# Position-bias lines of a hybrid decoder trunk: all heads in one matmul, sixteen partitions per head, written to memory in one transfer

## The chip, the cores and the metric

The kernel runs on one core of one Trainium2 chip. A core has a matrix engine (TensorE, PE in the tables, with its weight loads listed apart as PEld), a vector engine (DVE), a scalar engine (ACT), a GpSimd engine (POOL) and a queue processor that issues transfers (SP). 16 DMA engines move data between on-chip memory (SBUF) and HBM. The metric is the device time of one execution in microseconds; lower is better. Times "before" are the median of 3 runs.

## The reference

Two layers of a decoder trunk on 256 tokens of width 1024, all in float32: RMSNorm, one wide input projection, causal differential attention with 8 heads, a short gated convolution, an output projection, then a feed-forward part (dense in layer 0, 8 experts with top-2 routing in layer 1). The change concerns one small input of the attention, the relative-position bias, which depends only on the head and on the distance between query and key:

```python
dists = jnp.arange(S, dtype=jnp.int32)
bias_dist = rel_bias.astype(jnp.float32)[t5_causal_bucket(dists)].T      # (heads, 256)
...
dist = qpos[:, None] - kpos[None, :]
bias = bias_dist[:, jnp.maximum(dist, 0)]
s = jnp.einsum('bqhmd,bkhmd->bhmqk', qblk.astype(jnp.float32) * scale, kf)
s = s + bias[None, :, None]
s = jnp.where(dist >= 0, s, -jnp.inf)
p = jax.nn.softmax(s, axis=-1)
```

## The kernel before

**Weights and the main loop.** The weights stream through SBUF in pieces of 1 MB, called halves (128 partitions x 2048 float32). A mixer layer has 44 halves, numbered s = 0 to 43; two of them make the weights of one output unit (the first two units are the q and k columns of four heads). SP loads a half into one of RAW = 6 slots of `w_raw` (`load_half`, L359 to L362); from half 6 on it first waits for `lo_ready`, which says that the half six places back has been split. ACT copies a half to `w_hi` (L398) and DVE, or in two places POOL, subtracts to get `w_lo` (L407): a float32 product is made of three matmuls on the two parts (`product`, L411 to L413). There are SPLIT = 3 slots for the parts, so ACT splits half n only when PE has finished half n - 3 (`half_used`). PE takes 24 matmuls of 128x512 for a half (2 token tiles x 4 chunks x 3 products).

**What sets the order.** Everything is written out by hand, one program for each engine; engines meet only at semaphores. ACT's program of mixer step s begins with the split of half s + 2; then come copies of finished results from PSUM (L804 writes q to `rows` after half 1) and jobs of the attention. PE's program of step s is the 24 matmuls and then the jobs of table `JOBS`; the first is `turn_qk` 0 after half 2, eight transposes (L1660) of the `rows` that L804 writes, into banks 4 and 5.

**The bias.** It is made once, at the start of layer 0. SP loads `relb` (32 buckets x 8 heads) and `bucket` (33 x 384, one-hot: which bucket belongs to each of 384 distances; row 32 stands for masked places and carries -1e30). DVE copies `relb` to `relb_bc` in `v_buf`, each head's column repeated 128 times (L1551). After half 1, PE transposes the taps of the convolution (`conv_rows`, L1575, bank 4) and makes for each head one float32 matmul (L1583) of `relb_bc[:, h, :]` (33 x 128, all 128 columns alike) with `bucket`; the result is the line of 384 biases of that head, the same on all 128 partitions. Heads use banks 4 to 7 twice. ACT copies each line to `bias` (L714) and the taps to `convT` (L717); PE's matmul for head h, from head 4 on, waits until ACT has copied head h - 4 (`line_sb`). After four heads and after eight, ACT issues a transfer of 4 x 128 lines to the HBM tensor `lines` (L721), waits for the small sum of the lambdas (L724), and goes on. SP waits for both transfers (`line_out`, L494), then reads `lines` back with a skewed pattern (L496), so that partition p gets its line shifted by p, which is the bias tile of each head, and after that goes on with the load of half 8. The biases are first used at step 8 by DVE (L1171).

Of the kernel before, what the change touches and what calls it, by code (L numbers as in the profile page):

```python
# [26 lines left out]
P = 128  # L27
# [4 lines left out]
ACT = mybir.ActivationFunctionType  # L32
# [5 lines left out]
KC = D // P  # L38
HEADS = 8
HD = 64  # L40
NBUCKETS = 32
EPS = 1e-6
DEPTH = 2
# [12 lines left out]
WIDE = EXPERTS // 2  # L56
NARROW = P // 2
LINE = 384
BIG = 1e30

MIX_HALVES = 44
# [81 lines left out]
def build(nc, x, rel_bias, mix_norm_g, lam_qk, subln_g, conv_w, ffn_norm_g, router_w, final_norm_g,  # L143
          mix_slabs, dense_slabs, expert_slabs, bucket_of, out):
    lines = nc.dram_tensor("bias_lines", (HEADS, P, LINE), F32, kind="Internal").ap()
    with ExitStack() as ctx:
# [18 lines left out]
        part = sb("part", [P, TT * CHUNK])  # L165
        prob = sb("prob", [P, 2, LINE])
        wgt = sb("wgt", [P, LINE])
        wgtT = sb("wgtT", [P, LINE])
        arow = sb("arow", [P, TT, P])
        squares = sb("squares", [P, TT, P])  # L170

        with ExitStack() as trunk:
# [5 lines left out]
            v_buf = shared("v_buf", [P, KC * SEQ])  # L178
            bias = shared("bias", [P, HEADS, LINE])
            uT = shared("uT", [P, 4, SEQ + 2])  # L180
# [11 lines left out]
        relb = sb("relb", [64, HEADS])  # L192
        gsub = sb("gsub", [P, DEPTH, P])
        conv_rows = sb("conv_rows", [DEPTH * 3 * KC, P])
        convT = sb("convT", [P, DEPTH, 3, KC])
# [42 lines left out]
        bank = [ctx.enter_context(nc.psum_tensor(f"bank{b}", [P, CHUNK], F32)) for b in range(8)]  # L238
# [20 lines left out]
        gain = yT[:, :]  # L259
        yTv = yT[:, :].rearrange("p (c t) -> p c t", t=SEQ)  # L260

        relb_bc = v_buf[0:64, 0:HEADS * P].rearrange("b (h p) -> b h p", p=P)
        bucket = prob[0:NBUCKETS + 1, 0, :]
        lam_flat = k_buf[:, 0:DEPTH * 4 * HD]
        lamq = lam_flat.rearrange("p (l i d) -> p l i d", l=DEPTH, i=4)
# [25 lines left out]
        line_out, bias_in, out_sent = sem("line_out"), sem("bias_in"), sem("out_sent")  # L291
# [5 lines left out]
        conv_ps, conv_sb = sem("conv_ps"), sem("conv_sb")  # L297
        sum_ps = sem("sum_ps")
        line_ps, line_sb, relb_ready = sem("line_ps"), sem("line_sb"), sem("relb_ready")
# [178 lines left out]
        def _(sp):  # L478
# [12 lines left out]
            for s in range(3, RAW + 2):  # L491
                load_half(sp, s, mixer_source(0, s))

            sp.wait_ge(line_out, 16 * 2)  # L494
            for c0, j0, n in ((0, SEQ - 1, P), (P, SEQ - 1 - P, 2 * P)):
                sp.dma_start(bias[:, :, c0:c0 + n],  # L496
                             bass.AP(tensor=lines.tensor, offset=j0,
                                     ap=[[LINE - 1, P], [P * LINE, HEADS], [1, n]])).then_inc(bias_in, 16)
            for s in range(RAW + 2, MIX_HALVES):
# [209 lines left out]
        def _(act):  # L709
            def bias_lines():  # L710

                for h in range(HEADS):
                    act.wait_ge(line_ps, h + 1)
                    act.activation(bias[:, h, :], bank[4 + h % 4][:, 0:LINE], ACT.Copy).then_inc(line_sb, 1)  # L714
                    if h == 0:
                        act.wait_ge(conv_ps, 1)
                        act.activation(convT[:, :, :, :].rearrange("p l w c -> p (l w c)"),  # L717
                                       bank[4][:, LINE:LINE + DEPTH * 3 * KC], ACT.Copy).then_inc(conv_sb, 1)
                    if h % 4 == 3:
                        act.wait_ge(line_sb, h + 1)  # L720
                        act.dma_start(lines[h - 3:h + 1].rearrange("h p j -> p h j"),  # L721
                                      bias[:, h - 3:h + 1, :]).then_inc(line_out, 16)
                act.wait_ge(lam_sums, 1)
                act.activation(lam4[:, :, :], lam4[:, :, :], ACT.Exp).then_inc(lam_exp, 1)  # L724

# [364 lines left out]
        def _(dve):  # L1090
# [457 lines left out]
            chain(dve.memset(relb[NBUCKETS:64, :], -BIG))  # L1548
            norm(0)
            dve.wait_ge(relb_in, 16)  # L1550
            dve.tensor_copy(relb_bc, relb[:, :].unsqueeze(2).to_broadcast([64, HEADS, P])).then_inc(relb_ready, 1)  # L1551
            mixer(0)
            norm(1)
            dve.sem_inc(d_rows, 1)
# [15 lines left out]
        def _(pe):  # L1570
            def bias_lines():

                n = DEPTH * 3 * KC
                pe.wait_ge(conv_in, 16)
                pe.transpose(bank[4][:, LINE:LINE + n], conv_rows[:, :], ident[0:n, 0:n]).then_inc(conv_ps, 1)  # L1575
                pe.wait_ge(bucket_in, 16)
                pe.wait_ge(relb_ready, 1)
                for h in range(HEADS):
                    if h >= 4:
                        pe.wait_ge(line_sb, h - 3)  # L1580
                    if h == 4:
                        pe.wait_ge(conv_sb, 1)
                    pe.matmul(bank[4 + h % 4][:, 0:LINE], relb_bc[0:NBUCKETS + 1, h, :], bucket,  # L1583
                              start=True, stop=True).then_inc(line_ps, 1)

            def norm_turn(q, t):
                pe.wait_ge(hrow_ready, 2 * q + t + 1)
# [6 lines left out]
            def mixer(layer):  # L1594
# [15 lines left out]
                for s in range(MIX_HALVES):  # L1610
# [31 lines left out]
                    for job in JOBS[s]:  # L1642
                        kind, i = job
                        for b in JOB_BANKS[kind]:
                            if JOB_BEFORE[job, b]:
                                job_out(pe, layer, JOB_BEFORE[job, b])
                            elif layer:
                                job_out(pe, layer - 1, LAST_JOB[b])
                            else:
                                pe.wait_ge(line_sb, HEADS)  # L1650
                        head = HEADS * layer + i
                        if kind in ("turn_qk", "turn_u", "turn_b"):
                            if kind == "turn_u":
# [17 lines left out]
                        if kind == "scores":  # L1671
                            pe.wait_ge(qk_ready, 8 * layer + (4 if i < 4 else 8))
                            for m in range(2):
                                r = slice(HD * m, HD * m + HD)
                                pe.matmul(bank[4 + m][:, 0:P], qT[r, i, 0:P], kT[r, i, 0:P], start=True, stop=True)
                                pe.matmul(bank[4 + m][:, P:LINE], qT[r, i, P:SEQ], kT[r, i, 0:SEQ],
                                          start=True, stop=True).then_inc(bank_full[4 + m], 1)
# [5 lines left out]
                        if kind == "values":  # L1683
# [6 lines left out]
                                      stop=True).then_inc(bank_full[7], 1)  # L1690
# [345 lines left out]
```

## Time and profile before

| | us |
|---|---|
| median of 3 runs | 1773.92 |
| lowest, highest | 1771.62, 1774.75 |
| profiled execution | 1775.7 |
| its span, first to last instruction | 1774.0 |
| mean granted TensorE clock in it | 0.958 of full |
| TensorE busy in it | 1681.5 (95%) |

A profile is one execution, so sums are made against its span and carried over to the median as a difference. The granted clock is 1.00 for 2.4 GHz and 0.50 for 1.2 GHz. In a timeline each row gives start, duration, engine, line, operation, tile written and tiles read, shape and count; in square brackets stands the idle time of that engine before it and what ended it. Merged rows (x8 and the like) give the duration of the group; matmuls are pipelined, so the distance from one start to the next says more than a duration. A float32 matmul of the bias appears as two entries, so a row "x8" of L1583 is four heads.

### The profile page before, as it was taken

The numbers are of one execution on the slowest core, as the hardware profiler recorded it, in microseconds if no ns is written. First come the engines' busy times: TensorE is split into PE (matmuls) and PEld (weight loads), VectorE is DVE, ScalarE is ACT, GpSimd is POOL, SyncE is SP. The second block draws the span as 40 slices with busy tenths as digits, with TensorE's granted clock in tenths as the row PEclk, the third lists the DMA queues.
The fourth block names the chain that finished last, engine by engine and source line by source line (L and its number), as shares of the span: only waits on it lengthen the run. The fifth ranks groups of instructions, "written<-read, shape, count | busy, mean of one in ns | idle before, by whom it ended". The sixth has DMA issues, their size and how long they took to land.

```text
span 1774.0 us, 22510 instructions
## 1 busy us (share of the span) xinstructions
PE 1681.5 (95%) x7827; PEld 1390.1 (78%) x7827; DVE 1312.4 (74%) x1157; ACT 1118.5 (63%) x1120; POOL 202.9 (11%) x433
## 2 busy tenths in 40 slices
PE   6999999999989999979899989999899998999996
PEld 4888887888868888868687878888788877888784
DVE  4457756444454676667798989889898899888895
ACT  4456743434345567437577877778777788677784
POOL 1034331000000344128200000000000000000000
PEclk8999999999989999978999989999899999899997
DMA  6644454555535445536698989989989899999893
GB/s 271 251 167 165 177 184 150 194 182 184 188 137 176 157 166 180 189 140 266 244 420 343 407 360 370 376 335 398 421 336 380 338 374 422 361 371 369 340 400 127
DMA packets 71803, 488.67 MB, mean 275 GB/s; under 512 B 8667, under 2 KB 11948, under 8 KB 13228
## 3 DMA queue, kind: packets, MB, share of 16 engines
q1 hardware_dynamic: 69052, 483.89, 71.1%
q10 hardware_dynamic: 2672, 3.70, 0.6%
q8 instruction: 52, 0.85, 0.2%
q14 instruction: 27, 0.22, 0.0%
HBM read 484.94 MB, written 2.62 MB: 275 GB/s over the span
## 4 chain that ended last, share of the span: by engine, by line
PE 47%; DVE 8%; issue 7%; ACT 4%; POOL 3%; DMA 2%; DVEq 0%; ACTq 0%; SPq 0%; POOLq 0%
PE bank L411 13%; PE bank L413 12%; PE bank L412 12%; DVE w_lo L407 3%; DMA w_raw<-expert_slabs 2%; PE bank L1798 2%; DVE e_v L404 2%; PE bank L1819 2%; PE bank L1820 2%; ACT w_hi L398 2%; PE bank L1836 1%; DVE e_uy L407 1%; POOL wgtT L697 1%; PE bank L1826 1%; ACT hT L395 1%
## 5 line engine op out<-in xcount | busy, mean ns | idle before, releaser
L407 DVE TENSOR_TENSOR w_lo<-w_raw,w_hi 128x2048 fp32r<-128x2048 f32 x286 | 649.9, 2290 | 272.9 <-ACT w_hi L398 272.4
L398 ACT ACTIVATE w_hi<-w_raw 128x2048 fp32r<-128x2048 f32 x289 | 549.7, 1915 | 374.8 <-PE bank L413 362.8
L411 PE MATMUL bank<-w_hi,hT 128*128 128x512 f32 x912 | 365.0, 400 | 9.7 <-DVE hT L1132 8.9
L413 PE MATMUL bank<-w_hi,hT 128*128 128x512 f32 x912 | 359.0, 394 | 0.0
L412 PE MATMUL bank<-w_lo,hT 128*128 128x512 f32 x912 | 358.4, 393 | 0.0
L411 PEld LDWEIGHTS bank<-w_hi,hT 128*128 128x128 f32 x912 | 173.7, 190 | 47.9 <-DVE hT L1132 10.8
L413 PEld LDWEIGHTS bank<-w_hi,hT 128*128 128x128 f32 x912 | 173.2, 190 | 37.4
L412 PEld LDWEIGHTS bank<-w_lo,hT 128*128 128x128 f32 x912 | 174.0, 191 | 34.7
L407 DVE TENSOR_TENSOR e_uy<-w_raw,e_k 128x2048 fp32r<-128x2048 f32 x56 | 130.1, 2323 | 40.0 <-ACT e_k L398 40.0
L398 ACT ACTIVATE e_k<-w_raw 128x2048 fp32r<-128x2048 f32 x56 | 107.3, 1916 | 62.8 <-PE bank L413 33.6
L404 DVE TENSOR_TENSOR e_v<-w_raw,hT 128x2048 fp32r<-128x2048 f32 x55 | 125.8, 2287 | 16.4 <-ACT hT L395 16.1
L413 PE MATMUL bank<-w_hi,cT_lo 128*128 128x512 f32 x328 | 128.2, 391 | 0.0
L407 DVE TENSOR_TENSOR e_bias<-w_raw,e_q 128x2048 fp32r<-128x2048 f32 x55 | 125.6, 2283 | 2.8 <-ACT e_q L398 2.8
L398 ACT ACTIVATE e_q<-w_raw 128x2048 fp32r<-128x2048 f32 x55 | 105.6, 1920 | 14.9 <-PE bank L413 10.2
L395 ACT ACTIVATE hT<-w_raw 128x2048 fp32r<-128x2048 f32 x55 | 105.4, 1916 | 13.4 <-PE bank L413 6.6
L411 PE MATMUL bank<-w_hi,cT_hi 128*128 128x512 f32 x264 | 103.2, 391 | 1.5 <-DVE cT_lo L1278 1.5
L412 PE MATMUL bank<-w_lo,cT_hi 128*128 128x512 f32 x264 | 102.7, 389 | 0.0
L1836 PE MATMUL bank<-wgt,part 128*128 128x64 f32 x448 | 60.2, 293 | 22.5 <-DVE zero_r L1412 20.9
L1836 PEld LDWEIGHTS bank<-wgt,part 128*128 128x128 f32 x448 | 60.3, 211 | 26.9 <-issue 25.2
L413 PEld LDWEIGHTS bank<-w_hi,cT_lo 128*128 128x128 f32 x328 | 61.6, 188 | 13.5
L1819 PE MATMUL bank<-w_hi,hT 128*128 128x512 f32 x160 | 62.5, 391 | 0.1
L607 POOL TENSOR_SCALAR head_nw<-head_ss 128x2 f32<-128x2 f32 x16 | 6.1, 378 | 493.1 <-ACT squares L839 493.1
(340 smaller groups left out, 2815.5 us busy)
## 6 DMA issues: line engine op xcount, KB each, us to landing
w_raw<-expert_slabs SPq DMA_DIRECT2D x334, 1024.0 KB, 7.0
w_raw<-mix_slabs SPq DMA_DIRECT2D x88, 1024.0 KB, 4.8
w_raw<-dense_slabs SPq DMA_DIRECT2D x33, 1024.0 KB, 4.8
bias_lines<-bias ACTq DMA_DIRECT2D x2, 768.0 KB, 4.2
X<-in_x SPq DMA_DIRECT2D x2, 512.0 KB, 4.2
bias<-bias_lines SPq DMA_DIRECT2D x1, 1024.0 KB, 7.4
yT<-in_ffn_norm_g ACTq DMA_DIRECT2D x2, 512.0 KB, 5.4
v_buf<-expert_slabs SPq DMA_DIRECT2D x1, 1024.0 KB, 4.9
```

The source lines that it names most:

```text
L395: act.activation(hi_slot(n), in_pair(raw_of(n, early)), ACT.Copy).then_inc(hi_ready, 1)
L398: act.activation(hi_slot(n), raw_of(n, early), ACT.Copy).then_inc(hi_ready, 1)
L404: eng.tensor_tensor(in_pair(lo_slot(n)), in_pair(raw_of(n, early)), hi_slot(n), ALU.subtract).then_inc(lo_ready, 1)
L407: eng.tensor_tensor(lo_slot(n), raw_of(n, early), hi_slot(n), ALU.subtract).then_inc(lo_ready, 1)
L411: pe.matmul(dst, hi, whi, start=first, stop=False, skip_group_check=True)
L412: pe.matmul(dst, hi, wlo, start=False, stop=False, skip_group_check=True)
L413: return pe.matmul(dst, lo, whi, start=False, stop=last, skip_group_check=True)
L697: chain(pool.tensor_tensor(terms[:, :, c, :], src[:, r:r + 2, :], col_no[:, c:c + 1, :].to_broadcast([P, 2, 2 * EXPERTS]), ALU.mult))
L1798: ins = pe.matmul(bank[b][:, P * c:P * c + P], src[:, t, P * k:P * k + P], pick_r[:, t, :], start=t == 0, stop=t == TT - 1)
L1819: pe.matmul(dst, x, whi, start=first, stop=False, skip_group_check=True)
L1820: return pe.matmul(dst, x, wlo, start=False, stop=last, skip_group_check=True)
L1836: ins = pe.matmul(bank[2][:, at:at + NARROW], raw[:, P * j:P * j + P], fold[:, :], start=True, stop=True, skip_group_check=True)
```

## The change

The eight bias matmuls become one. `relb_bc` now repeats each head's column COPIES = 16 times, so that 8 heads x 16 copies fill the 128 columns of one weight tile; one matmul (bank 5) gives a tile in which partition 16h + r holds the line of head h. ACT makes one copy of it (128x384) into `bias[:, 0, :]` and issues one transfer in which each partition's line is read eight times and written to eight consecutive rows of `lines`: 16 partitions x 8 make the 128 rows of a head. `lines` ends with the contents that it had before. SP waits for one transfer. The copy of the convolution's taps now comes ahead of the line copy on ACT. PE's jobs that use banks 4 to 7 for the first time wait for the taps and for the one line copy.

```diff
--- before.py
+++ after.py
@@ -56,6 +56,7 @@
 WIDE = EXPERTS // 2
 NARROW = P // 2
 LINE = 384
+COPIES = P // HEADS
 BIG = 1e30
 
 MIX_HALVES = 44
@@ -259,7 +260,7 @@
         gain = yT[:, :]
         yTv = yT[:, :].rearrange("p (c t) -> p c t", t=SEQ)
 
-        relb_bc = v_buf[0:64, 0:HEADS * P].rearrange("b (h p) -> b h p", p=P)
+        relb_bc = v_buf[0:64, 0:P].rearrange("b (h r) -> b h r", r=COPIES)
         bucket = prob[0:NBUCKETS + 1, 0, :]
         lam_flat = k_buf[:, 0:DEPTH * 4 * HD]
         lamq = lam_flat.rearrange("p (l i d) -> p l i d", l=DEPTH, i=4)
@@ -491,7 +492,7 @@
             for s in range(3, RAW + 2):
                 load_half(sp, s, mixer_source(0, s))
 
-            sp.wait_ge(line_out, 16 * 2)
+            sp.wait_ge(line_out, 16)
             for c0, j0, n in ((0, SEQ - 1, P), (P, SEQ - 1 - P, 2 * P)):
                 sp.dma_start(bias[:, :, c0:c0 + n],
                              bass.AP(tensor=lines.tensor, offset=j0,
@@ -709,17 +710,14 @@
         def _(act):
             def bias_lines():
 
-                for h in range(HEADS):
-                    act.wait_ge(line_ps, h + 1)
-                    act.activation(bias[:, h, :], bank[4 + h % 4][:, 0:LINE], ACT.Copy).then_inc(line_sb, 1)
-                    if h == 0:
-                        act.wait_ge(conv_ps, 1)
-                        act.activation(convT[:, :, :, :].rearrange("p l w c -> p (l w c)"),
-                                       bank[4][:, LINE:LINE + DEPTH * 3 * KC], ACT.Copy).then_inc(conv_sb, 1)
-                    if h % 4 == 3:
-                        act.wait_ge(line_sb, h + 1)
-                        act.dma_start(lines[h - 3:h + 1].rearrange("h p j -> p h j"),
-                                      bias[:, h - 3:h + 1, :]).then_inc(line_out, 16)
+                act.wait_ge(conv_ps, 1)
+                act.activation(convT[:, :, :, :].rearrange("p l w c -> p (l w c)"),
+                               bank[4][:, LINE:LINE + DEPTH * 3 * KC], ACT.Copy).then_inc(conv_sb, 1)
+                act.wait_ge(line_ps, 1)
+                act.activation(bias[:, 0, :], bank[5][:, 0:LINE], ACT.Copy).then_inc(line_sb, 1)
+                act.wait_ge(line_sb, 1)
+                act.dma_start(lines.rearrange("h (r c) j -> (h r) c j", r=COPIES),
+                              bias[:, 0, :].unsqueeze(1).to_broadcast([P, P // COPIES, LINE])).then_inc(line_out, 16)
                 act.wait_ge(lam_sums, 1)
                 act.activation(lam4[:, :, :], lam4[:, :, :], ACT.Exp).then_inc(lam_exp, 1)
 
@@ -1548,7 +1546,7 @@
             chain(dve.memset(relb[NBUCKETS:64, :], -BIG))
             norm(0)
             dve.wait_ge(relb_in, 16)
-            dve.tensor_copy(relb_bc, relb[:, :].unsqueeze(2).to_broadcast([64, HEADS, P])).then_inc(relb_ready, 1)
+            dve.tensor_copy(relb_bc, relb[:, :].unsqueeze(2).to_broadcast([64, HEADS, COPIES])).then_inc(relb_ready, 1)
             mixer(0)
             norm(1)
             dve.sem_inc(d_rows, 1)
@@ -1575,13 +1573,8 @@
                 pe.transpose(bank[4][:, LINE:LINE + n], conv_rows[:, :], ident[0:n, 0:n]).then_inc(conv_ps, 1)
                 pe.wait_ge(bucket_in, 16)
                 pe.wait_ge(relb_ready, 1)
-                for h in range(HEADS):
-                    if h >= 4:
-                        pe.wait_ge(line_sb, h - 3)
-                    if h == 4:
-                        pe.wait_ge(conv_sb, 1)
-                    pe.matmul(bank[4 + h % 4][:, 0:LINE], relb_bc[0:NBUCKETS + 1, h, :], bucket,
-                              start=True, stop=True).then_inc(line_ps, 1)
+                pe.matmul(bank[5][:, 0:LINE], v_buf[0:NBUCKETS + 1, 0:P], bucket,
+                          start=True, stop=True).then_inc(line_ps, 1)
 
             def norm_turn(q, t):
                 pe.wait_ge(hrow_ready, 2 * q + t + 1)
@@ -1647,7 +1640,8 @@
                             elif layer:
                                 job_out(pe, layer - 1, LAST_JOB[b])
                             else:
-                                pe.wait_ge(line_sb, HEADS)
+                                pe.wait_ge(conv_sb, 1)
+                                pe.wait_ge(line_sb, 1)
                         head = HEADS * layer + i
                         if kind in ("turn_qk", "turn_u", "turn_b"):
                             if kind == "turn_u":
```

PE, after half 1 of the mixer of layer 0 (`bank` is PSUM, `w_hi`, `w_lo` weight parts, `hT` the normalised input, `conv_rows` the taps, `prob` the one-hot table, `v_buf` the repeated bias columns). Before:

```order
L413 MATMUL bank<-w_hi,hT 128x512
L1575 MATMUL bank<-ident,conv_rows 128x48 [waits conv_in]
L1583 MATMUL bank<-prob,v_buf 128x384 [waits relb_ready,bucket_in]
L1583 MATMUL bank<-prob,v_buf 128x384 x3
L1583 MATMUL bank<-prob,v_buf 128x384 [waits conv_sb,line_sb]
L1583 MATMUL bank<-prob,v_buf 128x384 [waits line_sb] x3
L411 MATMUL bank<-w_hi,hT 128x512 [waits lo_ready]
```

and the same place in the changed kernel:

```order
L414 MATMUL bank<-w_hi,hT 128x512
L1573 MATMUL bank<-ident,conv_rows 128x48 [waits conv_in]
L1576 MATMUL bank<-prob,v_buf 128x384 [waits relb_ready,bucket_in]
L412 MATMUL bank<-w_hi,hT 128x512 [waits lo_ready]
L413 MATMUL bank<-w_lo,hT 128x512
```

Seven bias matmuls and the two kinds of waits for ACT between them are gone from PE; half 2 stands right behind the one that is left.

ACT, between the split of halves 3 and 4 and the split of half 5 (`lam` the lambdas, `rows` the q rows that PE transposes next). Before:

```order
L398 ACTIVATE w_hi<-w_raw 128x2048 [waits half_used,landed4]
L714 ACTIVATE bias<-bank 128x384 [waits line_ps]
L717 ACTIVATE convT<-bank 128x48 [waits conv_ps]
L714 ACTIVATE bias<-bank 128x384 [waits line_ps] x3
L721 DMA bias_lines<-bias 128x4x384 [waits line_sb]
L714 ACTIVATE bias<-bank 128x384 [waits line_ps] x4
L721 DMA bias_lines<-bias 128x4x384 [waits line_sb]
L724 ACTIVATE lam<-lam 128x4 [waits lam_sums]
L804 ACTIVATE rows<-bank 128x512 [waits half_used]
L804 ACTIVATE rows<-bank 128x512
L398 ACTIVATE w_hi<-w_raw 128x2048 [waits half_used,landed5]
```

and the same place in the changed kernel:

```order
L399 ACTIVATE w_hi<-w_raw 128x2048 [waits half_used,landed4]
L714 ACTIVATE convT<-bank 128x48 [waits conv_ps]
L717 ACTIVATE bias<-bank 128x384 [waits line_ps]
L719 DMA bias_lines<-bias 1024x1x384 [waits line_sb]
L722 ACTIVATE lam<-lam 128x4 [waits lam_sums]
L802 ACTIVATE rows<-bank 128x512 [waits half_used]
L802 ACTIVATE rows<-bank 128x512
L399 ACTIVATE w_hi<-w_raw 128x2048 [waits half_used,landed5]
```

Seven copies and one issue are gone from ACT ahead of the two copies of `rows`; the one transfer that is left names 1024 rows of 384 on its written side.

## Rows read from the trace of the kernel before

**Rows 1.** Busy time of each engine by stretch, with granted clock and DMA share

```profile
core 0: us, PE busy (x) PEld busy (x) DVE busy (x) ACT busy (x) POOL busy (x), PEclk, DMA share, GB/s
...
30.25:33.00 2.75, 2.75 (x10) 1.48 (x9) 0.64 (x1) 2.58 (x2) 0.00 (x0) 1.00 0.00 0
33.00:40.13 7.13, 5.58 (x9) 2.49 (x8) 3.85 (x2) 4.22 (x9) 0.00 (x0) 0.50 0.31 112
40.13:47.15 7.02, 7.02 (x26) 5.62 (x26) 0.00 (x0) 1.67 (x4) 0.00 (x0) 0.78 0.53 159
...
60.00:288.00 228.00, 228.00 (x1109) 186.73 (x1108) 141.97 (x170) 127.56 (x211) 66.66 (x152) 1.00 0.50 176
...
865.00:1774.00 909.00, 865.88 (x4043) 722.91 (x4041) 809.88 (x538) 681.90 (x525) 0.00 (x0) 0.95 0.92 363
```

**Rows 2.** Timeline of PE, from the taps' transpose to half 3

```profile
30.25 0.26 PE L1575 MATMUL bank<-ident,conv_rows 48*128 48x48 f32 x1
30.36 2.84 PE L1583 MATMUL bank<-prob,v_buf 33*128 33x384 f32 x8
34.75 5.45 PE L1583 MATMUL bank<-prob,v_buf 33*128 33x384 f32 x8 [1.55 <-ACT convT L717]
40.13 0.79 PE L411 MATMUL bank<-w_hi,hT 128*128 128x512 f32 x1
...
43.51 0.40 PE L413 MATMUL bank<-w_hi,hT 128*128 128x512 f32 x1
...
47.15 1.03 PE L1660 MATMUL bank<-ident,rows 128*128 128x128 f32 x8
...
47.94 0.48 PE L411 MATMUL bank<-w_hi,hT 128*128 128x512 f32 x1
```

**Rows 3.** Timeline of ACT, 30 to 68 us

```profile
30.42 3.71 ACT L398 ACTIVATE w_hi<-w_raw 128x2048 fp32r<-128x2048 f32 x2 [4.93 <-PE bank L413]
...
34.41 0.20 ACT L717 ACTIVATE convT<-bank 128x48 f32<-128x48 f32 x1
34.50 1.25 ACT L714 ACTIVATE bias<-bank 128x384 f32<-128x384 f32 x3
35.78 0.42 ACTq L721 DMA_DIRECT2D bias_lines<-bias  x1
...
40.76 0.38 ACTq L721 DMA_DIRECT2D bias_lines<-bias  x1
...
41.30 1.07 ACT L804 ACTIVATE rows<-bank 128x512 f32<-128x512 f32 x2
...
65.52 1.92 ACT L398 ACTIVATE w_hi<-w_raw 128x2048 fp32r<-128x2048 f32 x1 [3.44 <-PE bank L413]
```

**Rows 4.** Granted clock and DMA rate in short stretches, columns as in Rows 1

```profile
33.00:33.20 0.20, 0.20 (x1) 0.00 (x0) 0.20 (x1) 0.20 (x1) 0.00 (x0) 0.51 0.00 0
...
37.00:38.00 1.00, 1.00 (x3) 0.47 (x2) 0.00 (x0) 0.32 (x1) 0.00 (x0) 0.50 0.95 352
...
43.20:43.40 0.20, 0.20 (x2) 0.12 (x1) 0.00 (x0) 0.00 (x0) 0.00 (x0) 0.89 1.05 376
```

**Rows 5.** Timeline of DVE: split of halves 3 and 4, first use of the bias

```profile
32.36 4.49 DVE L407 TENSOR_TENSOR w_lo<-w_raw,w_hi 128x2048 fp32r<-128x2048 f32 x2 [2.72 <-ACT w_hi L398]
...
82.62 1.15 DVE L1171 TENSOR_TENSOR prob<-bank,bias 128x384 f32<-128x384 f32 x2 [1.91 <-PE bank L1676]
```

**Rows 6.** Timeline of SP's queue: halves 3 to 7, bias read-back, halves from 8 on

```profile
6.00 14.10 SPq L362 DMA_DIRECT2D w_raw<-mix_slabs  x5
...
44.33 1.02 SPq L496 DMA_DIRECT2D bias<-bias_lines  x2
...
45.39 24.72 SPq L362 DMA_DIRECT2D w_raw<-mix_slabs  x7
```

**Rows 7.** Issue to landing of L721's two transfers, then by tile: half 8 alone

```profile
DMA to landing us min/median/max: 3.5/4.2/4.9
...
w_raw<-mix_slabs SPq DMA_DIRECT2D x1, 1024.0 KB, 9.3
```

## The prediction

> **What bounds the kernel now.** I read the table of busy time by stretch first [rows 1]. In the 228 us from 60 to 288 us, the rest of the first mixer, PE is busy throughout, at clock 1.00, while DVE, ACT and the DMA engines are busy for 142 us, 128 us and 50%: PE alone sets the pace. In the expert part (865 to 1774) PE is busy 866 of 909 us with the DMA engines at 0.92. Between 30 and 47 us it is otherwise. From 33.00 to 40.13 PE is busy 5.58 of 7.13 us at clock 0.50; from 40.13 to 47.15 it is busy throughout at 0.78. Then I read PE's timeline there [rows 2]. All of 30.36 to 40.13 goes to the bias matmuls: four heads in 2.84 us, a stop until 34.75 (the banks are full and ACT is still splitting halves 3 and 4 until 34.13 [rows 3]), four heads in 5.45 us at half the clock. The main matmuls of half 2 stand behind that on PE, in program order, and their weights have been ready for long: halves 3 and 4 are split by 36.85 [rows 5], half 2 before them. So the bias is on the path of the only engine that is short.
>
> **PE, the bias matmuls.** Seven of eight go. One head at full clock is 2.84 / 4 = 0.71 us from start to end; by the slow group it is 5.45 / 4 / 2 = 0.68 [rows 2]. The first bias matmul starts at 30.36, so half 2 can start at 31.04 to 31.07; the trace shows no float32 bias matmul followed by a main one at full clock, so I allow up to 0.1 for it and take 31.1 in place of 40.13. That is **9.0 us**, between 8.9 and 9.1. It holds only if half 2 waits for nothing else: DVE had been idle for 2.72 us when it began on half 3 at 32.36 [rows 5], so half 2 was split by 29.64, and the conv taps' wait is the same as before.
>
> **PE, the clock.** Half 2's 24 matmuls took 7.02 us (40.13 to 47.15), part of it at half clock. At full clock the distance is (47.15 - 43.51) / 16 = 0.2275 us, so 24 take 5.46, with some 0.1 for the first 5.55 [rows 2]. That is **1.45 us** more, if the clock stays up. The clock fell at 33.00, where PE was still running bias matmuls (the row from 30.25 to 33.00 has it busy all of 2.75 us, clock 1.00 [rows 1]; from 33.00 on it is 0.51 and 0.50 [rows 4]), and it came back between 43.20 and 43.40, 3.1 us after the main matmuls had begun, not during the 5.45 us of bias matmuls before. So in this trace bias matmuls neither kept the full clock nor brought it back, and now only 0.7 us of them stand between two runs of main matmuls. I take no fall. The Trainium skill (TensorE: Matmul & The Clock Gate, What's actually happening) lists idleness as what sends the engine back to the lower level. The trace does not agree as far as the fall at 33.00 goes, since PE was not idle then; by the page a fall would be out of the question in the changed kernel and the sum would be the same, by the row a small risk is left, which is priced among the rivals.
>
> **ACT, up to the q rows.** PE's `turn_qk` 0 behind half 2 needs the two copies at L804. Before, they began at 41.30, behind all of the bias, and cost PE nothing since they were done by 42.4, well ahead of 47.15. Now PE comes at 31.1 + 5.55 = 36.65. ACT is free of halves 3 and 4 at 34.13. Starts lie 0.09 apart behind the short taps' copy (34.41 to 34.50); the line copy is one of three that take 1.25, so at most 0.49; the issue 0.42; the little step on the lambdas and its gap lie within 41.30 - 41.14 = 0.16 behind the end of the second issue [rows 3]. 34.13 + 0.09 + 0.49 + 0.03 + 0.42 + 0.16 = 35.3, and the rows take 1.07: done at **36.4**, 0.25 us ahead of PE. I count nothing. If issuing the wider pattern took twice as long (0.84), ACT would be 0.1 late; that and a slower copy bound the cost at 0 to 0.5 us. It cannot be a gain, since PE then waits for nothing here anyway.
>
> **DVE, POOL.** The copy L1551 shrinks from 1024 to 128 columns, and DVE idles for 2.72 us before the split of half 3 anyway [rows 5]. Nothing. POOL's work is untouched.
>
> **The transfer, and SP behind it.** This is the one added cost that no row shows: a read of the same SBUF line eight times. The bytes are the same, 1.57 MB. SP waits for it, and behind that wait stand the read-back and the loads of half 8 and on. Bounds for the landing: 4.2 us, the median of one transfer of half the size, and 8.4, two such one after the other [rows 7]. The rate during the first was 352 GB/s [rows 4], so 1.57 MB take 4.5 us, and what is left of the quickest small one, 3.5 - 2.2 = 1.3, comes on top: I take 5.8. The issue moves from 40.76 (the second) to 34.74, so SP is free at 40.5 instead of 44.33 [rows 6]. That is 3.8 us earlier in the span, but PE is 10.4 us earlier, so 6.6 us of cover go. Half 8 is issued 1.06 behind the read-back's start and lands 9.3 later [rows 6, 7]: at 50.9. ACT splits it at 65.52 before [rows 3], 55.1 now. Cover left: **4.2 us**; at 8.4 us for the transfer still 1.6. Beyond that each microsecond costs one. The biases are needed at 82.62 - 10.4 = 72.2 [rows 5], over 20 us after the read-back. The sum has zero for all of this.
>
> At this place a rule of the Trainium skill speaks (DMA: Bandwidth & Descriptors, Rules for kernel authors): a transfer is spread over as many engines, up to 16, as the slowest dimension of both patterns allows, and a repeat of c copies as the outermost dimension confines it to c engines. Here partitions are outermost on the side that reads, and 1024 rows on the side that writes, so by the page all 16 engines work; if the eight copies counted as outermost it would be 8. No row shows either.
>
> **The sum.** 9.0 + 1.45 + 0 + 0 = 10.45, say **10.4 us** from the moment PE starts half 3 (47.94 before, 37.5 now). It stays to the end if all that follows hangs on PE: loads wait for splits, splits for `half_used`, and nothing is tied to absolute time. The span goes from 1774.0 to 1763.6. The profiled execution lies 1.8 above the median of the runs, of which 1.7 lies outside the span, so the difference carries over: 1773.9 - 10.4 = **1763.5 us**.
>
> **Rivals.**
>
> *The clock falls once all the same.* For: it fell at 33.00 with bias matmuls behind it [rows 1, 4], and now they still lie between 30.36 and 31.07. Against: they are a quarter of what they were before the fall. Price: if it falls at 33.0 and returns after as long as before, 3.1 us, half of that is lost, 1.55; with ACT late by 0.5 the time is 1765.5. Later stages have the clock at 0.95 [rows 1] and falls of their own, which this shift may move by a microsecond or two either way. Chance 0.11, with everything else that gives back 1.5 to 6 us.
>
> *The gain is hidden further on.* If the stream of expert weights (DMA 0.92 from 865 on) ran by itself, only PE's wait for it would grow and the time would be 1773.9. Against: every load waits for a slot that a split frees, and splits wait for PE, so the stream is shifted as a whole. Chance 0.03.
>
> *The transfer runs on few DMA engines, slower than before.* Price from the 4.5 us above: on 8 engines it lands after 9.0 + 1.3 = 10.3 us, half 8 is 0.3 late, 1763.8. On 4 it takes 19.3, half 8 is 9.3 late, 1772.8. On 2 it takes 37.3: 27.3 late, 16.9 more than the gain, **1790.8**. It decides from a landing time of 5.8 + 4.2 + 10.4 = 20.4 us, where the kernel is as slow as before. For: eight copies is a small dimension, and the pattern of reading one place eight times is in no row. Against: the partitions stay outermost, as in the old transfer. Chance of over 20 us 0.04.
>
> **How the numbers follow.** Forecast 0.82, clock or partial return 0.11, hidden 0.03, slow transfer 0.04. The low end is the forecast less what the fastest run of before lies under its median (2.3) and less 0.5 for ACT, clock and hop terms: 1760.7. The high end takes in the clock rival with ACT late (1765.5) and the run scatter above (0.8) with 0.5 more: 1766.8. Within 0.2% (3.5 us) counts as no change, about what a measurement of this kernel can tell. Faster by more: 0.93; same: 0.03 for the hidden gain and the 4-engine case; slower: 0.04.
>
> **What would show it.** In the changed kernel's PE timeline half 2 starts near 31.1 and half 3 near 37.5, and the stretch from 30 to 60 us has clock 1.00. ACT's q rows end before PE's transposes start. The transfer lands within 8.4 us of its issue, near 40.5, and ACT's wait before the split of half 8 still ends with PE, not with a DMA. From there every row of the first mixer stands 10.4 us earlier, as does the last instruction. A first split that waits for `w_raw`, or a clock of 0.50 in that stretch, would show me wrong.

## The result

| | median us | lowest to highest | ratio to before (95% interval) |
|---|---|---|---|
| before, in the runs beside it | 1772.30 | 1769.44 to 1774.75 (5 runs) | |
| changed | 1760.56 | 1759.81 to 1765.20 (5 runs) | 0.9943 (0.9931 to 0.9955) |

The change makes the kernel faster. The ratio, which is estimated by itself and is not the quotient of the medians, is 10.1 us of 1772.3, with 8.0 to 12.2 inside the interval; the forecast was 10.4. The medians lie 11.7 apart, and 1760.56 is 2.9 us below the forecast of 1763.5 and 0.14 us below the low end of its range. The profiled execution of the changed kernel took 1763.81 us, its span is 1762.0.

TensorE's timeline of the changed kernel (start, duration, engine, line, operation; it answers to [rows 2]):

```profile
30.95 0.26 PE L1573 MATMUL bank<-ident,conv_rows 48*128 48x48 f32 x1
31.04 0.87 PE L1576 MATMUL bank<-prob,v_buf 33*128 33x384 f32 x2
31.85 0.50 PE L412 MATMUL bank<-w_hi,hT 128*128 128x512 f32 x1
...
37.42 1.03 PE L1654 MATMUL bank<-ident,rows 128*128 128x128 f32 x8
38.22 0.48 PE L412 MATMUL bank<-w_hi,hT 128*128 128x512 f32 x1
```

From the taps' transpose to the start of half 2 it is 0.90 us instead of 9.88, and half 2 takes 5.57 (31.85 to 37.42) instead of 7.02. From the taps' transpose to half 3 it is 38.22 - 30.95 = **7.27 us**, against 47.94 - 30.25 = **17.69** before: 10.42 less. Half 3 itself stands only 9.72 earlier in the span, because this execution reached the taps 0.70 later; the start-up scatters by that much (30.57 to 31.42 in the profiles of eight of the experiments below, with all but the same code up to there). So I count from the taps on.

ACT's timeline of the changed kernel (answers to [rows 3]):

```profile
34.83 0.48 ACT L717 ACTIVATE bias<-bank 128x384 f32<-128x384 f32 x1
35.34 0.61 ACTq L719 DMA_DIRECT2D bias_lines<-bias  x1
...
36.12 1.07 ACT L802 ACTIVATE rows<-bank 128x512 f32<-128x512 f32 x2
37.68 1.92 ACT L399 ACTIVATE w_hi<-w_raw 128x2048 fp32r<-128x2048 f32 x1 [0.49 <-PE bank L414]
...
55.79 1.92 ACT L399 ACTIVATE w_hi<-w_raw 128x2048 fp32r<-128x2048 f32 x1 [3.44 <-PE bank L414]
```

The q rows are done at 37.19, 0.23 us before TensorE starts on them. Half 8 is split at 55.79 after 3.44 us of waiting for TensorE, the same wait as before: no weight load is late. SP's queue, the landing times, and the table by stretch (busy time of each engine, then granted clock, DMA share, GB/s):

```profile
41.99 1.02 SPq L497 DMA_DIRECT2D bias<-bias_lines  x2
43.06 22.77 SPq L363 DMA_DIRECT2D w_raw<-mix_slabs  x8
```

```profile
bias_lines<-bias ACTq DMA_DIRECT2D x1, 1536.0 KB, 6.6
...
w_raw<-mix_slabs SPq DMA_DIRECT2D x1, 1024.0 KB, 9.0
```

```profile
30.00:60.00 30.00, 30.00 (x140) 24.37 (x139) 13.93 (x8) 16.93 (x19) 0.00 (x0) 1.00 0.73 271
...
38.00:39.00 1.00, 1.00 (x9) 0.87 (x8) 0.00 (x0) 1.00 (x1) 0.00 (x0) 1.00 1.03 369
```

TensorE is busy for all of 30 to 60 us at clock 1.00, where before it had stretches at 0.50 and 0.78 [rows 1]. The transfer lands 6.6 us after its issue; in the slice from 38 to 39 us, while it runs, the 16 DMA engines are busy 1.03 on average.

### The profile page after: what moved, and what is told of

It is laid out like the page before. It is cut to its first block, busy times and chain, and to the rows that moved or that the text cites. A ratio compares the mean times of both kernels' runs of the same rounds, so it can differ in the third digit from the quotient of the medians.

```text
span 1762.0 us, 22475 instructions
## 1 busy us (share of the span) xinstructions
PE 1669.8 (95%) x7813; PEld 1384.2 (79%) x7813; DVE 1311.7 (74%) x1157; ACT 1116.5 (63%) x1113; POOL 205.6 (12%) x433
## 4 chain that ended last, share of the span: by engine, by line
PE 55%; DVE 6%; issue 5%; POOL 3%; ACT 2%; DMA 1%; DVEq 0%; ACTq 0%; POOLq 0%; SPq 0%
PE bank L412 13%; PE bank L414 13%; PE bank L413 12%; PE bank L1813 5%; PE bank L1814 5%; DVE w_lo L408 2%; PE bank L1830 2%; PE bank L1792 2%; ACT w_hi L399 1%; DVE e_v L405 1%; DVE e_uy L408 1%; POOL wgtT L698 1%; PE bank L1820 1%; DMA w_raw<-expert_slabs 1%; DVE e_bias L408 0%
```

## Experiments

The question is how the 10.42 us divide, and what in the sum was right only by luck. My theory: TensorE's work on the bias, its waits for ACT, and the low clock that came with both; the transfer is covered. Rivals: the waits were harmless and only the work counts; the clock has nothing to do with bias matmuls; the single transfer is the gain. All are edits of the changed kernel, but for the one that is an edit of the kernel before.

**Seven more bias matmuls, nobody waits for them.**

```diff
                 pe.matmul(bank[5][:, 0:LINE], v_buf[0:NBUCKETS + 1, 0:P], bucket,
                           start=True, stop=True).then_inc(line_ps, 1)
+                for _ in range(HEADS - 1):
+                    pe.matmul(bank[6][:, 0:LINE], v_buf[0:NBUCKETS + 1, 0:P], bucket, start=True, stop=True)
```

> The changed kernel with seven more copies of the bias matmul on TensorE right behind the one (into a bank that nothing reads yet; nobody waits for them, ACT and the transfer are as in the changed kernel). Half 3 starts at 38.2 in the changed kernel. Both theories: seven more cost 7 x 0.64 = 4.5 us at full clock. Theory A (a stretch of bias matmuls alone lets the clock fall, without any idling, as the fall at 33.00 in the kernel before suggests): the granted clock falls to 0.50 in that stretch or behind it, and half 3 starts at 44 to 46.5. Rival B (only the idling before 34.75 or chance brought the clock down): clock 1.00 throughout, half 3 at 42.7. If the time that TensorE spends is all that matters, the whole kernel is 4.5 (B) to 8 us (A) slower than the changed one, so 2 to 6 us faster than the kernel before.

**Twenty main matmuls of the same length in their place.**

```diff
+                pe.wait_ge(lo_ready, 3)
+                for _ in range(20):
+                    pe.matmul(bank[6][:, :], k_tok(hT_hi)[:, 0, 0:P], half_parts(2, 4, 0)[0], start=True, stop=True)
```

> The changed kernel with 20 main matmuls (128x512, the same tiles as half 2's first one, result never read) behind the bias matmul, 20 x 0.2275 = 4.55 us: the same length as the seven bias matmuls of the run beside it, but of the other kind. Theory A: clock 1.00 throughout and half 3 at 38.2 + 4.6 = 42.8, so it differs from its neighbour by the clock alone (1.3 to 3.7 us). Rival B: the same start of half 3 in both, within 0.3 us.

TensorE with seven more bias matmuls, then the table by stretch of the same run:

```profile
31.16 0.26 PE L1573 MATMUL bank<-ident,conv_rows 48*128 48x48 f32 x1
...
31.98 6.00 PE L1579 MATMUL bank<-prob,v_buf 33*128 33x384 f32 x14
37.91 0.79 PE L412 MATMUL bank<-w_hi,hT 128*128 128x512 f32 x1
...
46.20 0.48 PE L412 MATMUL bank<-w_hi,hT 128*128 128x512 f32 x1
```

```profile
33.00:35.00 2.00, 2.00 (x8) 1.19 (x7) 1.73 (x1) 2.00 (x3) 0.00 (x0) 1.00 0.04 8
35.00:36.00 1.00, 1.00 (x4) 0.55 (x3) 1.00 (x2) 0.52 (x3) 0.00 (x0) 0.59 0.00 0
...
38.00:41.00 3.00, 3.00 (x7) 2.38 (x8) 0.00 (x0) 0.00 (x0) 0.00 (x0) 0.50 1.03 372
...
42.00:43.00 1.00, 1.00 (x6) 0.82 (x5) 0.00 (x0) 0.00 (x0) 0.00 (x0) 1.00 0.43 25
```

and with the main matmuls as filler:

```profile
30.57 0.26 PE L1573 MATMUL bank<-ident,conv_rows 48*128 48x48 f32 x1
...
31.47 4.83 PE L1580 MATMUL bank<-w_hi,hT 128*128 128x512 f32 x20
...
42.37 0.48 PE L412 MATMUL bank<-w_hi,hT 128*128 128x512 f32 x1
```

```profile
34.00:38.00 4.00, 4.00 (x20) 3.30 (x19) 3.17 (x2) 2.11 (x6) 0.00 (x0) 1.00 0.45 163
```

Theory A held. In the first run TensorE is never idle from 31 to 43, and the granted clock falls in the slice 35 to 36, inside the bias matmuls, and is back in 42 to 43, some 4 us after the main matmuls began. With main matmuls in the same place it stays at 1.00. Half 3 starts 46.20 - 31.16 = 15.04 us behind the taps in the first run and 42.37 - 30.57 = 11.80 in the second. So the same length of work costs 4.53 us as main matmuls (11.80 - 7.27) and 7.77 as bias matmuls: **3.24 us** are the clock. In these two runs it is the kind of matmul that decides, not a gap. Which property of the bias matmuls it is (33 rows of weights, float32, 384 columns) is not shown: all three differ at once from the main matmuls.

**TensorE waits for ACT once, behind its one bias matmul.**

```diff
+                pe.wait_ge(conv_sb, 1)
+                pe.wait_ge(line_sb, 1)
```

> The changed kernel, but TensorE waits behind its one bias matmul until ACT has copied taps and line (as the kernel before waited in the middle). ACT's copies end at 35.3, so half 2 starts at 35.4 instead of 31.85: 3.5 us of idling. Theory (waits for ACT and the clock that they cost were part of the price): half 3 starts 3.5 us later at full clock, 41.8, or 43 to 43.6 if the clock falls in the idling. Rival (the waits were hidden or cost nothing; the gain is from the number of matmuls alone): no more than 0.5 us later. The whole kernel: 3.5 to 5.5 us slower than the changed one by the theory.

```profile
31.42 0.26 PE L1573 MATMUL bank<-ident,conv_rows 48*128 48x48 f32 x1
...
35.87 0.76 PE L412 MATMUL bank<-w_hi,hT 128*128 128x512 f32 x1 [3.48 <-ACT convT L714]
...
43.65 0.48 PE L412 MATMUL bank<-w_hi,hT 128*128 128x512 f32 x1
```

Half 2 starts after 3.48 us of idling, and half 3 starts 43.65 - 31.42 = 12.23 us behind the taps, 4.96 more than in the changed kernel. 3.48 is the wait, 1.48 is a fall of the clock at its end (0.92 from 35.3 to 35.6 us, 0.50 behind that, 0.69 on average from 34 to 38). The rival, by which such waits are free, is out. What is left of the 10.42 after 4.53 (work) and 3.24 (clock) is **2.65 us**: the 1.55 that TensorE stood still before 34.75 [rows 2], and 1.1 for the longer time at half clock that came with the stop; this last share is a remainder and not measured by itself. All three shares are differences taken in this order; the stop and the clock act on each other, so another order could move a part from one to the other.

**Kernel before, with one transfer for its eight lines.**

```diff
-            sp.wait_ge(line_out, 16 * 2)
+            sp.wait_ge(line_out, 16)
...
-                    if h % 4 == 3:
-                        act.wait_ge(line_sb, h + 1)
-                        act.dma_start(lines[h - 3:h + 1].rearrange("h p j -> p h j"),
-                                      bias[:, h - 3:h + 1, :]).then_inc(line_out, 16)
+                act.wait_ge(line_sb, HEADS)
+                act.dma_start(lines.rearrange("h p j -> p h j"), bias[:, :, :]).then_inc(line_out, 16)
```

> The kernel before (eight bias matmuls, eight copies), with the two transfers of the lines replaced by one of all eight heads behind the eighth copy. It tells the transfer apart from the rest. Theory (the transfer is covered in either kernel): same time as before within 1 us; the one transfer lands about 6.6 us after its issue near 40.8, SP goes on at 47.5 instead of 44.3, and ACT still never waits for a weight load. Rival (the single transfer is where the gain comes from): 3 us or more faster.

```profile
46.85 1.02 SPq L496 DMA_DIRECT2D bias<-bias_lines  x2
```

```profile
bias_lines<-bias ACTq DMA_DIRECT2D x1, 1536.0 KB, 5.7
```

The first row is SP's queue, the second the time to landing. The ratio to before is 0.9996 (0.9986 to 1.0006), and from the taps to half 3 it is 48.35 - 30.64 = 17.71 us, as before. SP is freed at 46.85 instead of 44.33, and nothing later comes late for it. The number of transfers is not the gain.

**Changed kernel, its transfer in two.**

```diff
-            sp.wait_ge(line_out, 16)
+            sp.wait_ge(line_out, 16 * 2)
...
-                act.dma_start(lines.rearrange("h (r c) j -> (h r) c j", r=COPIES),
-                              bias[:, 0, :].unsqueeze(1).to_broadcast([P, P // COPIES, LINE])).then_inc(line_out, 16)
+                for g in range(2):
+                    act.dma_start(lines.rearrange("h (r c) j -> (h r) c j", r=COPIES)[:, 4 * g:4 * g + 4, :],
+                                  bias[:, 0, :].unsqueeze(1).to_broadcast([P, 4, LINE])).then_inc(line_out, 16)
```

> The changed kernel with its one transfer in two (four copies of each line each), issued one behind the other on ACT. Issue: 0.42 + 0.42 instead of 0.61 us, so ACT's q rows are ready 0.25 us later and TensorE waits 0 to 0.3 us more. Landing of the second some 6.8 us after the first issue, as for the one. Same time as the changed kernel within 1 us; a difference of 2 us or more would mean that the number of transfers matters by itself.

```profile
35.56 0.97 ACTq L720 DMA_DIRECT2D bias_lines<-bias  x2
...
36.69 1.07 ACT L803 ACTIVATE rows<-bank 128x512 f32<-128x512 f32 x2
```

```profile
37.91 1.07 PE L1655 MATMUL bank<-ident,rows 128*128 128x128 f32 x8
```

The issues take 0.97 together, not 0.84; taps to half 3 is 38.73 - 31.17 = 7.56, 0.29 more than with one. The ratio is 0.9943 (0.9922 to 0.9963), the same as the changed kernel's.

**Three spare transfers ahead of the one, on ACT.** The spares write to HBM tensors that nobody reads.

```diff
...
+                for spare in spares:
+                    act.dma_start(spare.rearrange("h (r c) j -> (h r) c j", r=COPIES),
+                                  bias[:, 0, :].unsqueeze(1).to_broadcast([P, P // COPIES, LINE])).then_inc(line_out, 16)
...
-            sp.wait_ge(line_out, 16)
+            sp.wait_ge(line_out, 16 * 4)
```

> The changed kernel with three more transfers of the same 1.57 MB (to HBM tensors that nobody reads) ahead of the one, and SP waiting for all four: landing after some 4 x 4.2 + 2.3 = 19 us instead of 6.6, SP free at about 54.7 instead of 42.0, half 8 in SBUF at about 65 instead of 52. ACT splits half 8 at 55.8 in the changed kernel. Theory of the prediction (cover ends there, each microsecond beyond costs one): all later work is about 9 us late, the kernel is at 1770 to 1772, about as before. Rival (behind the split there are two steps, some 6.6 us, before TensorE needs half 8): TensorE loses 2 to 4 us only.

ACT's queue, ACT and TensorE in this run:

```profile
35.22 3.88 ACTq L721 DMA_DIRECT2D spare<-bias  x3
39.13 4.22 ACTq L723 DMA_DIRECT2D bias_lines<-bias  x1
...
43.51 1.06 ACT L806 ACTIVATE rows<-bank 128x512 f32<-128x512 f32 x2
```

```profile
44.72 1.94 PE L1658 MATMUL bank<-ident,rows 128*128 128x128 f32 x8 [7.25 <-ACT rows L806]
```

The time, ratio 0.9984 (0.9972 to 0.9995), would fit the prediction's theory, but the rows say that it came from elsewhere: ACT was held at the issue, 3.88 us for the three spares and 4.22 for the fourth transfer, and TensorE waited 7.25 us for the q rows. The run does not test the cover. The next two do.

**Two and four spare transfers on SP, each waited for, ahead of the read-back.**

```diff
...
             sp.wait_ge(line_out, 16)
+            for i, spare in enumerate(spares):
+                sp.dma_start(spare.rearrange("h (r c) j -> (h r) c j", r=COPIES),
+                             bias[:, 0, :].unsqueeze(1).to_broadcast([P, P // COPIES, LINE])).then_inc(line_out, 16)
+                sp.wait_ge(line_out, 16 * (i + 2))
```

> The changed kernel, but SP, freed by the bias transfer, sends two spare transfers of 1.57 MB to HBM tensors that nobody reads, one after the other, each waited for, before it reads the lines back. ACT is untouched (the run with three spares on ACT's queue held ACT itself at the issue for 8 us, so it did not test the cover). Each spare takes some 6.6 us, so half 8 lands at 52.1 + 13.2 = 65.3; ACT splits it at 55.8 in the changed kernel. Theory of the prediction (beyond that instant each microsecond costs one): everything after is 9.5 us late, the kernel is as slow as before. Rival (TensorE needs half 8 only two steps after ACT starts on it, about 66.3, and the two splits take 4.2, so 6.6 us more are covered): 2.9 us late.

> The same with four spare transfers: half 8 lands at 52.1 + 26.4 = 78.5. Theory of the prediction: 22.7 us late, the kernel 12 us slower than before. Rival: 16.1 us late, 5 to 6 us slower than before. The biases are read back at about 68.4 + 7.1 = 75.5 against a need at 72.9, which is inside either delay.

ACT's split of half 8 and TensorE's first matmul on it, with two spares:

```profile
64.33 1.92 ACT L400 ACTIVATE w_hi<-w_raw 128x2048 fp32r<-128x2048 f32 x1 [12.34 <-DMA w_raw<-mix_slabs]
```

```profile
68.72 0.47 PE L413 MATMUL bank<-w_hi,hT 128*128 128x512 f32 x1 [2.50 <-DVE w_lo L409]
```

and with four:

```profile
77.04 1.91 ACT L400 ACTIVATE w_hi<-w_raw 128x2048 fp32r<-128x2048 f32 x1 [24.41 <-DMA w_raw<-mix_slabs]
```

```profile
81.42 0.76 PE L413 MATMUL bank<-w_hi,hT 128*128 128x512 f32 x1 [14.54 <-DVE w_lo L409]
```

The rival held. Counted from the taps, ACT splits half 8 with two spares 33.76 us behind them against 24.84 in the changed kernel, 8.9 late, and TensorE loses 2.50; with four it is 21.0 late, and TensorE loses 14.54. There are some 6.5 us more of cover than the prediction counted (8.9 - 2.50 and 21.0 - 14.54): TensorE works on halves 6 and 7 while half 8 is split.

**The bias in the gap of half 1.** Taps and bias matmul stand between the two token tiles of half 1, where TensorE waits for the second tile; DVE's copy L1549 moves ahead accordingly.

```diff
...
                                 ins = half(s, (t,), (2, 3))
+                                if layer == 0:
+                                    bias_lines()
...
-                    if s == 1 and layer == 0:
-                        bias_lines()
```

> The changed kernel with the taps' transpose and the bias matmul moved on TensorE to the place between the two token tiles of half 1, where TensorE waits for the second tile of the normalised input (0.4 to 0.6 us idle there in both kernels); DVE copies the repeated bias columns in its idle time ahead of that. Theory: the 0.9 us between half 1 and half 2 go (half 2 follows at once), 0.5 us of work are hidden in the gap, 0.3 to 0.4 are not; half 3 starts 0.5 us earlier counted from TensorE's first matmul. By the times that can't be told from the changed kernel (0.03%).

**The same, and ACT copies the q rows before it issues the transfer.**

```diff
                 act.wait_ge(line_ps, 1)
                 act.activation(bias[:, 0, :], bank[5][:, 0:LINE], ACT.Copy).then_inc(line_sb, 1)
+                act.wait_ge(half_used, 2)
+                for t in range(TT):
+                    act.activation(tok_c(rows)[:, t], bank[t][:, :], ACT.Copy, scale=HD ** -0.5).then_inc(act_rows, 1)
                 act.wait_ge(line_sb, 1)
...
-                        if kind in ("conv", "attn", "wo"):
+                        if kind in ("conv", "attn", "wo") or u == layer == 0:
...
```

> The run with the bias in the gap of half 1, with one more edit: ACT makes the two copies of the q rows ahead of the issue of the bias transfer and of the step on the lambdas, not behind. In the run with the bias in the gap alone, TensorE waited 0.87 us for those copies, and from the second transposes of the norm to the transposes of q it took 15.29 us against 14.76 in the changed kernel. Theory (the only thing late there was ACT): 14.4 us, no wait ahead of the transposes of q. Rival (the gap hides less than it seems): 14.8 or more. In the whole time 0.3 us can't be told.

TensorE in the first and in the second of them:

```profile
38.41 1.06 PE L1654 MATMUL bank<-ident,rows 128*128 128x128 f32 x8 [0.87 <-ACT rows L802]
```

```profile
37.38 1.07 PE L1657 MATMUL bank<-ident,rows 128*128 128x128 f32 x8
```

The first missed: the bias work now stands ahead of the signal that half 1 is done, so ACT starts on halves 3 and 4 later (9.08 us behind the norm's second transposes, against 8.45 in the changed kernel) and comes late with the q rows; from the norm's second transposes to those of q it is 15.29 us against 14.76 in the changed kernel. With the rows first it is 37.38 - 22.97 = 14.41, as expected, without a wait. Both ratios, 0.9945 (0.9932 to 0.9959) and 0.9933 (0.9915 to 0.9952), can't be told from the changed kernel's. In the timeline the gap saves 0.35 us (14.76 - 14.41), but only with the q rows ahead of the issue on ACT.

The runs side by side, without the two with the bias in the gap, whose taps stand elsewhere. "To half 3" counts from the taps' transpose; the next column adds its difference from the changed kernel to the changed kernel's 10.42 us of gain (for the two runs with spares on SP the difference comes later, and is TensorE's wait for half 8):

| run | to half 3, us | against before by the timeline, us | measured ratio (interval) | in us |
|---|---|---|---|---|
| changed | 7.27 | -10.4 | 0.9943 (0.9931 to 0.9955) | -10.1 |
| seven more bias matmuls | 15.04 | -2.6 | 0.9977 (0.9966 to 0.9988) | -4.1 |
| main matmuls as filler | 11.80 | -5.9 | 0.9956 (0.9941 to 0.9972) | -7.8 |
| half 2 waits for ACT | 12.23 | -5.5 | 0.9979 (0.9966 to 0.9993) | -3.7 |
| kernel before, one transfer | 17.71 | 0.0 | 0.9996 (0.9986 to 1.0006) | -0.7 |
| changed, two transfers | 7.56 | -10.1 | 0.9943 (0.9922 to 0.9963) | -10.1 |
| three spares on ACT | 15.48 | -2.2 | 0.9984 (0.9972 to 0.9995) | -2.8 |
| two spares on SP | | -7.9 | 0.9971 (0.9959 to 0.9983) | -5.1 |
| four spares on SP | | +4.1 | 1.0031 (1.0020 to 1.0042) | +5.5 |

All intervals but that with two spares (3.0 to 7.3 us faster) hold the value that the timeline gives. In that run's own profile the first mixer ends 7.6 us closer to the taps than in the kernel before, as the timeline has it; why the median shows less is not shown.

## Why the prediction was right

**The bias matmuls, 9.0 us.** Measured 9.88 - 0.90 = 8.98. The mechanism was named as work, a stop and half clock, and the runs divide the whole 10.42 into 4.53 of work, 3.24 of clock and 2.65 of the stop and what follows it.

**The clock, 1.45 us.** Measured 7.02 - 5.57 = 1.45, and no fall. That bias matmuls bring the clock down without idling, as the fall at 33.00 suggested, is now shown by the run with seven more of them. The Trainium skill (TensorE: Matmul & The Clock Gate, What's actually happening) gives idleness, in its table of the two states, as what sends the engine back to the lower level. In the run in which half 2 waits the clock did fall in the idling, but in the run with seven more bias matmuls it fell with TensorE busy throughout (1.00 in every slice from 31 to 43 us), which that table does not name; the measurement decides.

**ACT, 0.25 us of cover.** Measured 0.23, with both sides a little later than taken: ACT by 0.09, though the issue alone took 0.61 us and not 0.42, TensorE by 0.07, since one bias matmul and the hop to half 2 took 0.81 and not 0.74. The prediction left one thing out: where TensorE does come too early for the rows, it starts 0.15 us after ACT's end and not at once (37.76 to 37.91 with the transfer in two, 38.26 to 38.41 with the bias in the gap). So the real cover was 0.23 - 0.15 = 0.08, and that zero was the right count was partly luck. The transfer in two shows it: its issues held ACT 0.36 us longer, and half 3 started 0.29 later, which is 0.36 less those 0.08 to within 0.01.

**The transfer.** 6.6 us, inside the bounds of 4.2 and 8.4, but 0.8 over the value taken. The same bytes from eight different lines, in the kernel before with one transfer, took 5.7, close to the 5.8 taken. The rest is not simply the price of the eight-fold repeat. The issue is 0.2 us longer (0.61 against 0.42), and that goes with the repeat. But the landing varies by more: 6.6 in the changed kernel and four of the runs, and 6.0 in both runs with filler on TensorE, whose transfer is the same; with the q rows copied first it was 7.8.

```profile
bias_lines<-bias ACTq DMA_DIRECT2D x1, 1536.0 KB, 6.0
```

That row is from the run with seven more bias matmuls. The bulk flows at the same rate with and without the repeat (mostly 361 to 392 GB/s, in slices of 0.2 us); in the changed kernel it is through by 41.0 us and a trickle of 15 to 90 GB/s follows until 41.6, which both runs with filler lack. So against the one run without the repeat the landing takes 0.3 to 0.9 us longer. What makes the trickle is open. The transfer stays covered. All 16 DMA engines worked (1.03 busy), so the rule cited from the Trainium skill agrees with the trace.

**The cover of half 8: this step failed.** "Beyond that each microsecond costs one" counted up to ACT's split and not up to the engine that bounds. Measured, 3.7 us of cover up to the split (landed at 43.06 + 9.0 = 52.1, needed 55.8), and behind it the 6.5 of the two steps that TensorE has before it needs half 8. The sum did not depend on it, since the cover held, but the slow rival was priced too high: the kernel would have been as slow as before only from a landing time of some 27 us (6.6 + 3.7 + 6.5 + 10.4, an estimate), not 20.4.

**To the end.** Up to the end of the first mixer the gain is kept: DVE's first row of the next norm in the kernel before and in the changed one,

```profile
297.50 1.29 DVE L1115 SCALAR_TENSOR_TENSOR q_buf<-X,nwi,yT 128x1024 f32<-128x1024 f32 x1
```

```profile
287.81 1.28 DVE L1113 SCALAR_TENSOR_TENSOR q_buf<-X,nwi,yT 128x1024 f32<-128x1024 f32 x1
```

stand 267.25 and 256.86 us behind the taps, 10.39 apart, where half 3 had 10.42. Behind that, the distance of the two profiled executions in the span moves: from 9.7 us here to 8.6 behind the next joint of two stages, some 8 to 11 in the expert part, 12.0 at the last norm. So the last sign of the prediction, the last instruction 10.4 us earlier, did not come: it is 12.0. Such a joint in the kernel before and the same place in the changed one:

```profile
303.00:306.00 3.00, 3.00 (x9) 2.35 (x8) 2.82 (x6) 0.00 (x0) 2.01 (x1) 0.50 0.03 5
```

```profile
293.30:296.30 3.00, 1.97 (x9) 1.28 (x7) 2.76 (x8) 0.00 (x0) 1.79 (x1) 1.00 0.05 11
```

In the first the clock was down while TensorE made the first matmuls of the dense part, in the second it came down a little later, in a wait. That such differences change from run to run, and are no effect of the change, is seen in the kernel before with one transfer: its profile is at the same place as the kernel before at the end of the first mixer (267.28 us behind the taps), and 6.8 us ahead of it at the last norm. The five runs of the changed kernel go from 1759.8 (clock 0.966) to 1765.2 (0.960). This scatter is enough to explain why the median passed the range's low end, which was hung on one median of three: the median of the kernel before beside these runs was itself 1.6 lower. By the same scatter, that 10.1 comes so near to the 10.4 of the forecast is in part luck: the interval goes from 8.0 to 12.2. The timeline's 10.42 up to half 3 is the better evidence.

## What to carry to other kernels

Small operations on the bounding engine can cost more than their length: here 4.5 us of them cost 7.8 with the clock that they brought down, and 10.4 with a stop for another engine in their middle, so cut their number before moving them. Lay independent small problems side by side on the partitions of one tile, and let a transfer make the copies. Count the cover of a transfer up to the engine that bounds, through every step between, and before asking what a late transfer costs, look which engine the issue itself holds.

## What was new about the hardware

- The granted clock fell while TensorE was busy without a gap, in a run of float32 bias matmuls with 33 rows of weights (0.59 in the slice in which it fell, then 0.50), and did not fall with main matmuls in the same place. Which of their properties matters is open.
- The issue of a transfer can hold its engine when several others are under way: of four of 1.57 MB in a row in ACT's queue, the issues took 0.61, 0.68, 2.52 and 4.22 us. A single issue with the eight-fold repeat took 0.61 us, with the four or eight different lines of the kernel before 0.38 to 0.42. One transfer of half the size ahead did little (0.42 and 0.52, the transfer in two).
- The clock column says 1.00 at the start-up, where the distance of the matmuls is that of the lower level. In the changed kernel:

```profile
16.00:24.00 8.00, 7.74 (x29) 6.30 (x30) 0.28 (x2) 0.70 (x2) 4.27 (x4) 1.00 1.03 425
```

```profile
18.57 0.63 PE L414 MATMUL bank<-w_hi,hT 128*128 128x512 f32 x1
18.99 0.63 PE L412 MATMUL bank<-w_hi,hT 128*128 128x512 f32 x1
...
21.28 0.40 PE L412 MATMUL bank<-w_hi,hT 128*128 128x512 f32 x1
21.52 0.39 PE L413 MATMUL bank<-w_lo,hT 128*128 128x512 f32 x1
```

  Starts lie 0.42 us apart at 18.57, as in stretches at 0.50, and 0.24 at 21.28. At the start of a trace, go by the distance of the matmuls.
